# Turning the second feed-forward's gate and up values by transposing DMAs of 16-bit halves instead of on TensorE

## The reference, cut to what matters

```python
D_FF_2 = 5632

def causal_dwconv(u, w, b):
    """u: [B,S,C]; w: [CONV_W,C]; out[t] = sum_j w[j] * u[t-(CONV_W-1)+j] + b."""
    S = u.shape[1]
    up = jnp.pad(u, ((0, 0), (CONV_W - 1, 0), (0, 0)))
    out = b
    for j in range(CONV_W):
        out = out + up[:, j:j + S] * w[j]
    return out

# the end of second_block
h2 = rmsnorm_2(x, norm2_g[l])
u = causal_dwconv(jnp.einsum('bsd,df->bsf', h2, w_up[l]), conv_w[l], conv_b[l])
u_gate, u_val = u[..., :D_FF_2], u[..., D_FF_2:]
x = x + jnp.einsum('bsf,fd->bsd', jax.nn.silu(u_gate) * u_val, w_down[l])
```

## Time and profile before

| What | Value |
|---|---|
| median of 3 runs | 2542.74 us |
| the profiled execution | 2542.45 us |
| its span | 2540.7 us |
| TensorE busy | 2533.9 us, 11596 matmuls |
| VectorE busy | 1413.6 us |
| ScalarE busy | 1229.0 us |
| GpSimd busy | 138.8 us |
| read from memory | 467.44 MB, 185 GB/s over the span |

### The profile page before, as it was taken

One profiled execution on the slowest core, in us unless ns is written; L12 is line 12 of the kernel. 1 busy time (PEld: TensorE's weight loads), 2 busy tenths in 40 slices (PEclk: granted clock), 3 DMA queues, 4 the chain that ended last, 5 costly groups with the idle time before them and its releaser, 6 DMA issues.

```text
span 2540.7 us, 33424 instructions
## 1 busy us (share of the span) xinstructions
PE 2533.9 (100%) x11596; PEld 2099.3 (83%) x11596; DVE 1413.6 (56%) x1707; ACT 1229.0 (48%) x1698; POOL 138.8 (5%) x211
## 2 busy tenths in 40 slices
PE   9999999999999999999999999999999999999999
PEld 7888888888888888888888888888888888888887
DVE  5555555555555555555455555565566646665665
ACT  6555445444344434455444544544555445553553
POOL 2222200000000000000000111100000000000000
PEclk9999999999999999999999999999999999999999
DMA  8555556665666566666666666655666566666665
GB/s 239 161 171 161 169 173 185 191 189 189 193 190 189 190 192 190 191 198 190 179 185 179 182 185 179 184 176 189 184 182 190 190 192 187 178 193 195 184 189 166
DMA packets 327827, 471.16 MB, mean 185 GB/s; under 512 B 23232, under 2 KB 126244, under 8 KB 327584
## 3 DMA queue, kind: packets, MB, share of 16 engines
q1 hardware_dynamic: 326352, 467.30, 61.3%
q0 software_dynamic: 1088, 2.07, 0.3%
q10 hardware_dynamic: 272, 0.26, 0.0%
HBM read 467.44 MB, written 2.11 MB: 185 GB/s over the span
## 4 chain that ended last, share of the span: by engine, by line
PE 99%; DMA 0%; SPq 0%; DVE 0%; ACT 0%; issue 0%
PE ps L473 32%; PE ps L475 32%; PE ps L474 31%; PE ps L922 1%; PE ps L722 1%; PE ps L567 0%; PE ps L549 0%; PE ps L582 0%; PE ps L555 0%; PE ps L756 0%; PE ps L639 0%; PE ps L659 0%; PE ps L888 0%; DMA raw<-in_w_in 0%; PE ps L592 0%; PE ps L863 0%
## 5 line engine op out<-in xcount | busy, mean ns | idle before, releaser
L1395 DVE TENSOR_TENSOR w_lo<-raw,w_hi 128x1024 fp32r<-128x1024 f32 x880 | 1081.1, 1230 | 1078.6 <-ACT w_hi L976 1076.5
L976 ACT ACTIVATE w_hi<-raw 128x1024 fp32r<-128x1024 f32 x880 | 931.3, 1060 | 1182.3 <-PE ps L475 1172.9
L473 PE MATMUL ps<-w_hi,xT_hi 128*128 128x512 f32 x2204 | 873.3, 396 | 0.5 <-DVE xT_lo L1414 0.5
L475 PE MATMUL ps<-w_hi,xT_lo 128*128 128x512 f32 x2204 | 859.8, 390 | 0.0
L474 PE MATMUL ps<-w_lo,xT_hi 128*128 128x512 f32 x2204 | 858.3, 389 | 0.0
L473 PE MATMUL ps<-w_hi,yT_hi 128*128 128x512 f32 x1312 | 515.2, 393 | 0.0
L475 PE MATMUL ps<-w_hi,yT_lo 128*128 128x512 f32 x1312 | 511.2, 390 | 0.0
L474 PE MATMUL ps<-w_lo,yT_hi 128*128 128x512 f32 x1312 | 510.6, 389 | 0.0
L475 PEld LDWEIGHTS ps<-w_hi,xT_lo 128*128 128x128 f32 x2204 | 413.7, 188 | 87.2
L473 PEld LDWEIGHTS ps<-w_hi,xT_hi 128*128 128x128 f32 x2204 | 414.0, 188 | 85.9 <-issue 2.7
L474 PEld LDWEIGHTS ps<-w_lo,xT_hi 128*128 128x128 f32 x2204 | 414.2, 188 | 82.9
(11 more groups left out here) (204 smaller groups left out, 899.7 us busy)
## 6 DMA issues: line engine op xcount, KB each, us to landing
raw<-in_w_up SPq DMA_DIRECT2D x264, 512.0 KB, 3.7
raw<-in_w_down SPq DMA_DIRECT2D x176, 512.0 KB, 3.8
raw<-in_w_in SPq DMA_DIRECT2D x160, 512.0 KB, 3.8
raw<-in_w_gate SPq DMA_DIRECT2D x88, 512.0 KB, 3.7
raw<-in_w_out SPq DMA_DIRECT2D x60, 512.0 KB, 3.7
raw<-in_w_in SPq DMA_DIRECT2D x128, 192.0 KB, 2.8
raw<-in_w_in SPq DMA_DIRECT2D x192, 128.0 KB, 2.5
raw<-in_w_proj_m SPq DMA_DIRECT2D x16, 512.0 KB, 3.8
```

The costliest lines, as they stand in the source:

```text
L473: pe.matmul(o, hi[:, q], w_hi[n % NS][:, k, 0:width], start=first, stop=False)
L475: mm = pe.matmul(o, lo[:, q], w_hi[n % NS][:, k, 0:width], start=False, stop=last)
L976: nc.scalar.activation(w_hi[n % NS][:, :, 0:width], raw[n % NS][:, :, 0:width], ACT.Copy).then_inc(hi_ready, 1)
L1395: v.tensor_tensor(w_lo[n % NS][:, :, 0:width], raw[n % NS][:, :, 0:width], f32(w_hi[n % NS][:, :, 0:width]), ALU.subtract).then_inc(lo_rea ...
```

## The change

The transposes of `turn_u` are gone from TensorE, and the four PSUM banks with them. In their place, for each of the 22 results:

- GpSimd splits `tok_u[g]`, one token tile at a time, into the low and high 16-bit halves of its values (`halve`, two copies of 1024 16-bit values a partition), as soon as ScalarE has written the tile.
- ScalarE's queue issues, right behind the two copies out of PSUM, two transposing DMAs, one for each token tile, each when its tile is halved (`send_across`). One moves 128 x 1024 16-bit values, 256 KB, from SBUF to SBUF.
- GpSimd waits for both, and for VectorE's last tap on the result before (`landed` and the wait on `conv_step`), and joins the halves to 32-bit values in `turned` (`join`, two copies of 1024 16-bit values a partition).
- The convolution's taps on ScalarE and VectorE read `turned` in SBUF, where they read PSUM. Where they stand in the two programs is not changed.

The SBUF tiles `prob`, `mix`, `pT`, `y` and `stage` of earlier phases become parts of one tile `work`, and the halves, the turned halves and the joined values lie over them. ScalarE's loop over the rounds is written out instead of looped.

```diff
-        stage = sb("stage", [NT, 2, P])
+        work = sb("work", [12 * S])
+        prob, mix, pT = (work[:, c0 * S:c1 * S] for c0, c1 in ((0, 4), (4, 6), (6, 8)))
+        y = work[:, 8 * S:10 * S].rearrange("p (t n) -> p t n", t=NT)
+        stage = work[:, 10 * S:12 * S].rearrange("p (t c n) -> p t c n", t=NT, c=2)
+        halves = work[:, 0:4 * S].bitcast(U16).rearrange("p (t e n) -> p t e n", t=NT, e=2)
+        flipped = work[:, 4 * S:8 * S].bitcast(U16).rearrange("p (e f s) -> p e f s", e=2, s=S)
+        turned = work[:, 8 * S:12 * S].rearrange("p (f s) -> p f s", s=S)
+        turned_halves = work[:, 8 * S:12 * S].bitcast(U16).rearrange("p (n e) -> p n e", e=2)
...
-            def turn_u(g, fg, i):
-
-                pe.wait_ge(by_act, at(i, FREE + PH["ffn2_up0"][BY_ACT] + 4 * fg + 2 * g + 2, 4))
-                pe.wait_ge(act_lo, at(i, FREE + 4 * fg, 4))
-                for f in range(4):
-                    for t in range(NT):
-                        mm = pe.transpose(ps[4 + 2 * g + f // 2][:, f % 2 * S + t * P:f % 2 * S + (t + 1) * P],
-                                          tok_u[g][:, t, f * P:(f + 1) * P], ident[:])
-                mm.then_inc(tok_u_T[g], 1)
...
+            def send_across(i, k, step=0):
+
+                for t in range(NT):
+                    act.wait_ge(halved, at(i, 2 * k + t + 1, 2 * step))
+                    act.dma_start_transpose(flipped[:, :, :, t * P:(t + 1) * P].rearrange("p e f s -> p (e f) s"),
+                                            halves[:, t, :, :].rearrange("p e n -> p (e n)")).then_inc(across, 16)
...
                         evac(up, i, g, tok_u[g], 0, W, rstd)
+                        send_across(i, TURNS["ffn2"] + 2 * fg0 + g, 2)
...
-                            nc.scalar.activation(z[:, f, :], ps[4 + 2 * g + f // 2][:, f % 2 * S:(f % 2 + 1) * S], ACT.Identity,
+                            nc.scalar.activation(z[:, f, :], turned[:, f, :], ACT.Identity,
...
-                    with act.Fori(1, n_fg) as i:
+                    for i in range(1, n_fg):
...
-                        v.scalar_tensor_tensor(z[:, f, j:S], ps[4 + 2 * g + f // 2][:, c0:c0 + S - j], w, z[:, f, j:S],
+                        v.scalar_tensor_tensor(z[:, f, j:S], turned[:, f, 0:S - j], w, z[:, f, j:S],
...
+            def halve(z, t):
+
+                g_.tensor_copy(halves[:, t, :, :], z[:, t, :].bitcast(U16).rearrange("p (n e) -> p e n", e=2)).then_inc(halved, 1)
+
+            def join(b):
+
+                c = slice(b * 2 * S, (b + 1) * 2 * S)
+                return g_.tensor_copy(turned_halves[:, c, :], flipped.rearrange("p e f s -> p (f s) e")[:, c, :])
+
+            def landed(i, k, step=0):
+                pool.wait_ge(across, at(i, 32 * (k + 1), 32 * step))
...
+            pool.wait_ge(kt_lo, 5 * KT)
+            fg0 = 0
+            for t, width in enumerate(THIRDS):
+                for i in range(width // W):
+                    for g in range(2):
+                        for tt in range(NT):
+                            pool.wait_ge(by_act, at(i, FREE + PH[f"ffn2_up{t}"][BY_ACT] + 2 * g + tt + 1, 4))
+                            halve(tok_u[g], tt)
+                        landed(i, TURNS["ffn2"] + 2 * fg0 + g, 2)
+                        pool.wait_ge(conv_step, at(i, 16 * fg0 + 8 * g, 16))
+                        join(0)
+                        join(1).then_inc(tok_u_T[g], 1)
+                fg0 += width // W
```

More of the change, by code:

```diff
@@ L25 @@
 X = mybir.AxisListType.X
+U16 = mybir.dt.uint16
 P = 128
@@ L136, in evacuated @@
     return FREE + PH[name][1] + 2 * (3 * (head // 4) + groups[head % 4])
+TURNS, turns_ = {}, 0
+for name_, n_ in (("ffn2", 22),):
+    TURNS[name_], turns_ = turns_, turns_ + n_
 def at(i, c, step):
@@ L293, in two_blocks @@
             "ffn_scale", "tok_tanh_ready", "tok_T", "tok_hi", "tok_lo"))
+        halved, across = sem("z_halved"), sem("z_across")
         tanh_ready, silu_step, act_hi, act_lo = sem("tanh_ready"), sem("silu_step"), sem("act_hi"), sem("act_lo")
@@ L938, in behind @@
                             turn_x(3, 4 * KT)
-                        if u == 8:
-                            turn_u(0, fg0, 0)
                     up_turn(0, behind)
                     with pe.Fori(1, n_fg) as i:
[L943 to L952, removed]
+                        up_turn(i, nothing)
                     def act_ready(u):
@@ L957, in ffn2 @@
                         if t == 2 and i == 0:
-                            early_groups(down, units, xT, None, act_ready, first)
+                            early_groups(down, units, xT, None, act_ready, nothing)
                             continue
@@ L961, in ffn2 @@
                             group(down, i, 2 * units, g, units, xT, 0, evac_free(by_dve, down, BY_DVE, i, g), ready=act_ready,
-                                  behind=first if i == 0 else nothing, halves=t == 2 and i == 1 and g == 1)
+                                  halves=t == 2 and i == 1 and g == 1)
                     fg0 += n_fg
@@ L1823, in tap @@
                         w = conv[:, ds(at(i, 4 * fg0 + f + g * (CONV_T // 2) + (2 - j) * CONV_T, 4), 1)]
-                        c0 = f % 2 * S
-                        v.scalar_tensor_tensor(z[:, f, j:S], ps[4 + 2 * g + f // 2][:, c0:c0 + S - j], w, z[:, f, j:S],
+                        v.scalar_tensor_tensor(z[:, f, j:S], turned[:, f, 0:S - j], w, z[:, f, j:S],
                                                ALU.mult, ALU.add).then_inc(conv_step, 1)
```

## The result

The changed kernel takes 2613.36 us (median of 4, 2605.93 to 2615.84) against 2542.74: a ratio of 1.0272, 95% interval 1.0259 to 1.0285, so 70.6 us slower. The direction was forecast, the size was not: 2566 was predicted, and the loss is three times as large as the +23.7 of the sum. The time lies inside the stated range of 2522 to 2685 us, but by luck: its upper part was set for a slower transfer (L = 16), not for what happened.

A forecast was written before the change was run, and what follows sets the result against it. TensorE was taken to bound the kernel, holding 99% of the last chain. From 2542.45 us, 42.8 us of waits against 19.1 saved gave +23.7, so 2566 us; range 2522 to 2685.

The forecast's parts named there:

- L: Landing of both transposing DMAs, counted from ScalarE's split behind the result's last unit: 3.1 + T = 10.8 us forecast.
- Removed work: On TensorE, 176 transposes of line 922 go: 22 results x 0.87 us = 19.1 us, all that can be won.
- GpSimd: Halving and joining copies: 1.04 us each, halves ready at 3.1 and 4.15 us, joins beside an idle VectorE.
- Rival 4: GpSimd is the slow part: halves and joins take twice 1.04 us, 77 us on top, 2643 us; chance 0.04.
- The transfer: Transposing DMAs from first issue to landing of both: paced like the gate columns' short runs, 7.7 us.
- T: Time from the first transposing DMA's issue to both landing: 7.7 us, including 0.5 for the first issue.
- Rival 1: Transposing DMAs go at plain pace, T = 3.8: 2524 us, at most 2537.6; chance 0.33.
- rival 3: Transfer chokes, going by written runs, T = 22.5: 368 us of waits, 2892 us; chance 0.10 with all beyond T = 12.
- What is queued behind: Splits behind ScalarE's late first tap make TensorE wait: 9 x 2.6 + 2 x 4.2 + 11 x 1.0 = 42.8 us.
- so each result pays its own wait: In the eight units, 21.8 us, between two results ScalarE and VectorE catch up, so lateness does not carry over.
- signs of being wrong: DMAs landing within 6 us, GpSimd copies far from 1.04 us, ScalarE held in the issue, or `raw` later than splits want.
- Loads hidden: Weight loads, issued when VectorE frees a slot, land 3.7 us later, wanted four units later: no cost counted.

## Why the prediction was right or wrong, point by point

- **Removed work: right.** 19.1 us forecast, 19.8 measured.
- **GpSimd: right in kind, a little low.** Halving alone takes 1.04 us (the minimum of 44), as taken; a join takes 1.15 alone and up to 2.16 beside VectorE. I had the joins beside an idle VectorE. In the change VectorE works off held splits just then, and the pair takes 2.3 to 3.5 us instead of 2.2. The taps start at 13.9 us on average instead of 13.0. Rival 4 is out: it wanted twice 1.04 for each copy.
- **The transfer: right in the mean, partly by luck.** T was the most open step. It was taken from the pace of short runs on the read side, and the queue's packets speak for that count: 46736 less the 272 that were there before are 1056 for each of 44 DMAs, some 8 x 128. L came out at 10.9 for 10.8. But the mean joins two groups, 9.7 for the gate and 12.1 for the up values, and the term inside T was too small: 2.6 us of all engines were forecast, 4.0 were taken. Rival 1 (plain pace) and rival 3 (written runs, 25.6) are out. A result's 512 KB took 4.0 us of all 16 engines (3.4% of 2613 us over 22 results), while the weights' 467.30 MB took 57.8%, which is 1.7 us for 512 KB. The forecast cited the Trainium skill for rival 1 (Advanced Engine Details and Errata, section X-Bar Transpose (TRN2)): transposing DMAs are as fast as regular ones. That does not hold here: they cost 2.4 times as much engine time for each byte.
- **What is queued behind: the step that failed.** It rests on "so each result pays its own wait" and on 0.5 us for the issue. The issue took 2.8 to 5.0 us for a pair, 4.5 in the median: 1.25 to 1.7 for the first DMA and 1.5 to 3.6 for the second. Why the second holds the engine for so long is not shown; the DMA engines were full in the short ones as in the long ones. I had read the row that hints at this, the 3.69 us of the second gate-column issue, and used it for rival 3 only, though the forecast named a hold in the issue and a late `raw` as signs of being wrong. Both came. The two splits behind the issue are then late before the tap is, the weights' loads that follow VectorE come late in turn (26.3 us of waits for `raw`), and every second result starts with ScalarE already behind: the landings of the up values come at 10.2 to 15.0 us, those of the gate at 8.4 to 11.0. So of the 63.6 us of waits the nine up values have 34.2 (23.4 forecast), the two ends of thirds 15.1 (8.4) and the gate's results 14.3 (11.0). On SyncE's queue the same sum held within 3 us (42.8 forecast, 40.0 measured): 23.9, 10.4 and 5.7. So it was right there for the up values, near for the ends, and twice too high for the gate, whose DMAs landed at 9.6 us and not at 10.8.
- **The clock: not in the sum at all.** 19.5 us on top of the waits, more than a quarter of the loss, and some 7 at the edges of the waits. I named no term for what TensorE loses after it has waited. The clock fell nine times in the second feed-forward, each time in or just behind one of the ten waits of 2.14 us and more. One of these ten, of 2.15 us, and the sixteen shorter ones (up to 1.86 us) had no fall behind them. In three of the other runs waits of 1.9 to 2.2 us were followed by one, but not all such waits.
- **Loads hidden: wrong.** Their 3.7 us are hidden only as long as VectorE frees the slots on time; ScalarE's splits waited 26.3 us for `raw`, and 55.3 with the DMAs on SyncE's queue.

Beginning and end of the account: 23.7 forecast = 42.8 - 19.1. Measured 70.6: the waits became 63.6 where ScalarE is held, and 19.5 of clock and some 7 at the edges of the waits came on top.

## What to carry to other kernels

Where work moves from a bounding engine to a path of several engines, count two latencies apart: when the result is there, and how long each engine on the path is held, its DMA issue included. An instruction that waits for the new path has to be moved in its own engine's program to where the result will be, and with it what hangs on it; here that, the right queue and the order of the down phases turned +71 us into -19. A wait of TensorE costs more than its length: some 0.27 us at its edges here, and the lower clock in or behind most waits over 2 us. Put a price on that before a sum ends near zero.

## What the runs showed of the hardware that was not expected

- A transposing DMA of 128 x 1024 16-bit values holds its queue's engine for 1.25 us at least and 1.5 in the median in the change, up to 3.6 there and up to 4.2 in other runs, on ScalarE's queue and on SyncE's alike; a plain load of 512 KB held SyncE 0.37 us. In the 4.32 us of one pair's issue the DMA engines were 98% busy, but they were as full in one of the shortest second issues (1.55 us), so full engines alone do not explain the long ones:

```profile
1824.76:1829.08 4.32, 4.32 (x21) 3.58 (x20) 0.00 (x0) 0.00 (x0) 0.95 (x1) 1.00 0.98 161
2121.70:2123.25 1.55, 1.55 (x8) 1.31 (x7) 0.00 (x0) 0.00 (x0) 0.00 (x0) 1.00 1.04 318
```

- The taps gained nothing by reading SBUF instead of PSUM: ScalarE's took 587 ns in the median against 558 before, VectorE's 479 against 473.
- GpSimd's copy of 1024 16-bit values, strided on one side, takes 1.04 us to halve and 1.15 us to join, as long as one of 1024 32-bit values.
